# The up weights of an expert in two transfers of 4 MB, in place of four of 2 MB

## The reference

```python
def expert_block(args):            # for each expert with its tokens
    xb = t[tk]
    uu = xb @ w_up[eid] + b_up[eid]            # w_up (32, 1024, 2048)
    glu = jnp.minimum(uu[:, :D_FF], 7.0)
    lin = jnp.clip(uu[:, D_FF:], -7.0, 7.0)
    act = glu * jax.nn.sigmoid(1.702 * glu) * (lin + 1.0)
    yb = act @ w_down[eid] + b_down[eid]       # w_down (32, 1024, 1024)
    return yb * wt[:, None]
```

## Time and profile before

| | |
|---|---|
| time, median of 3 runs (lowest to highest) | 1246.54 us (1245.84 to 1250.47) |
| the profiled execution's own time | 1254.68 us |
| its span, first to last instruction | 1252.9 us |
| mean granted TensorE clock | 0.971 |
| TensorE busy | 1187.5 us, 95% of the span |
| VectorE, ScalarE, GpSimd busy | 408.7, 303.2, 36.5 us |
| moved by DMA | 442.27 MB, 353 GB/s over the span |
| queue q1 (SyncE), q10 (ScalarE) | 312.75 MB, 125.85 MB |

### The profile page before, as it was taken

How to read it: one execution, slowest core, us unless ns; L and a number is a source line. 1 busy time by engine, 2 the same in 40 slices (tenths; PEclk the granted TensorE clock), 3 DMA queues, 4 the chain that set the end, 5 groups by cost and what they waited for, 6 DMA issues and landing times.

```text
span 1252.9 us, 14792 instructions
## 1 busy us (share of the span) xinstructions
PE 1187.5 (95%) x5802; PEld 574.4 (46%) x5802; DVE 408.7 (33%) x732; ACT 303.2 (24%) x479; POOL 36.5 (3%) x90
## 2 busy tenths in 40 slices
PE   5999999998999999999999999899998999999984
PEld 3788879896333333333333333333333333333321
DVE  3543676723223132332313133132223131313233
ACT  6454244513111112111111221111111111111212
POOL 2001600000000000000000000000000000000000
PEclk9899999997999999999999999999999999999996
DMA  8650515368899999999999999999999999999971
GB/s 304 225 206 1 168 37 185 135 269 338 354 387 431 426 427 429 431 428 427 427 428 431 429 428 427 428 429 430 428 427 428 428 431 427 428 427 427 429 331 43
DMA packets 49841, 442.27 MB, mean 353 GB/s; under 512 B 3915, under 2 KB 16787, under 8 KB 25200
## 3 DMA queue, kind: packets, MB, share of 16 engines
q1 hardware_dynamic: 40032, 312.75, 60.6%
q10 hardware_dynamic: 8720, 125.85, 23.6%
q0 software_dynamic: 1056, 3.21, 0.7%
HBM read 438.06 MB, written 3.73 MB: 353 GB/s over the span
## 4 chain that ended last, share of the span: by engine, by line
PE 90%; DMA 3%; DVE 2%; ACT 1%; another core or an unknown queue 1%; issue 1%; POOL 0%; SPq 0%; DVEq 0%; POOLq 0%
PE ps L443 35%; PE ps L457 18%; PE ps L333 15%; PE ps L420 7%; DMA regionB<-in_w_up 3%; PE ps L464 2%; PE ps L450 2%; PE ps L465 2%; PE ps L426 1%; PE ps L435 1%; PE ps L1712 1%; PE ps L1497 1%; PE ps L1669 1%; PE ps L1728 1%
## 5 line engine op out<-in xcount | busy, mean ns | idle before, releaser
L443 PE MATMUL ps<-regionB,regionP 128*64 128x512 f32 x1024 | 243.2, 618 | 14.1 <-DMA regionB<-in_w_up 14.1
L443 PE MATMUL ps<-regionA,regionP 128*64 128x512 f32 x1024 | 225.9, 598 | 6.5 <-DMA regionA<-in_w_up 5.6
L457 PE MATMUL ps<-regionD,regionP 128*64 128x512 f32 x992 | 224.7, 595 | 0.0
L701 DVE TENSOR_TENSOR regionP<-ps,regionP 128x512 f32<-128x512 f32 x32 | 22.1, 691 | 403.6 <-PE ps L426 403.6
L443 PEld LDWEIGHTS ps<-regionA,regionP 128*64 128x64 f32 x1024 | 72.1, 137 | 149.0 <-issue 138.0
L443 PEld LDWEIGHTS ps<-regionB,regionP 128*64 128x64 f32 x1024 | 70.0, 141 | 150.9 <-issue 133.6
L457 PEld LDWEIGHTS ps<-regionD,regionP 128*64 128x64 f32 x992 | 68.5, 137 | 129.6 <-issue 129.5
L695 DVE SCALAR_TENSOR_TENSOR roundedP<-regionP,roundedP 64x512 fp32r<-64x512 f32 x64 | 45.2, 746 | 183.4 <-ACT roundedP L594 183.4
L420 PE MATMUL ps<-regionP 128*64 128x512 f32 x384 | 90.5, 607 | 2.4 <-ACT regionP L1153 2.4
L609 ACT ACTIVATE regionP<-ps 128x512 f32<-128x512 f32 x31 | 18.5, 597 | 298.8 <-PE ps L420 298.8
L735 DVE TENSOR_TENSOR regionP<-ps,regionP 128x1024 f32<-128x1024 f32 (+1 forms) x48 | 58.5, 1219 | 97.1 <-PE ps L465 84.9
(11 more groups left out here) (280 smaller groups left out, 1165.6 us busy)
## 6 DMA issues: line engine op xcount, KB each, us to landing
regionA<-in_w_up SPq DMA_DIRECT2D x64, 2048.0 KB, 41.9
regionB<-in_w_up SPq DMA_DIRECT2D x64, 2048.0 KB, 42.0
regionD<-in_w_down ACTq DMA_DIRECT2D x60, 2048.0 KB, 14.4
regionA<-in_w_in SPq DMA_DIRECT2D x4, 2048.0 KB, 14.1
regionB<-in_w_mk SPq DMA_DIRECT2D x4, 1024.0 KB, 9.2
regionD<-in_w_mv SPq DMA_DIRECT2D x4, 1024.0 KB, 21.6
regionD<-in_w_out SPq DMA_DIRECT2D x4, 1024.0 KB, 12.9
regionD<-in_w_mq SPq DMA_DIRECT2D x4, 1024.0 KB, 5.0
```

The costliest lines, as they stand in the source:

```text
L443: ins = pe.matmul(ps[64 * half:64 * half + 64, n_, :], XTe[:, k % 4, k // 4, :], w[:, k, 1024 * half + 512 * n_:1024 * half + 512 * n_ + 512],
L457: ins = pe.matmul(ps[64 * n_:64 * n_ + 64, 6, :], lin[:, k, :], w[:, k, 512 * n_:512 * n_ + 512], start=(k == 0), stop=(k == KT - 1))
```

## The change

The loads of an expert's up weights are issued in halves: four blocks of rows each, 4 MB, which are 32 KB for every partition, in place of four pieces of two blocks, 2 MB and 16 KB. A half is issued when both chunks that read its place are done, and TensorE waits for a half before its first chunk of the two. The wait on `down_done` before the last expert's pieces is gone. The loads ahead of the loop keep their four pieces, but two of them count on one semaphore, so that TensorE waits for 32 there. The overflow part is changed in the same way.

```diff
@@ moe_sync
-                for c_ in range(4):
-                    if isinstance(e, int) and e == E - 3 and c_ == 1:
-
-                        sp.wait_ge(S("down_done"), e * 2)
-                    sp.wait_ge(S("up_done"), e * 4 + c_ + 1)
-                    sp.dma_start((upA, upB)[h][:, 2 * c_:2 * c_ + 2, :], up_src(e + 2)[:, 2 * c_:2 * c_ + 2, :]
+                for c_ in range(2):
+                    sp.wait_ge(S("up_done"), e * 4 + 2 * c_ + 2)
+                    sp.dma_start((upA, upB)[h][:, 4 * c_:4 * c_ + 4, :], up_src(e + 2)[:, 4 * c_:4 * c_ + 4, :]
                                  ).then_inc(S(f"up{'AB'[h]}_in{c_}"), 16)
...
@@ moe_tensor
                 for c_ in range(4):
-                    pe.wait_ge(S(f"up{'AB'[h]}_in{c_}"), (pair + 1) * 16)
+                    if c_ % 2 == 0:
+                        pe.wait_ge(S(f"up{'AB'[h]}_in{c_ // 2}"), (pair + 2) * 16)
                     up_product(pe, (upA, upB)[h], 2 * c_, 2).then_inc(S("up_done"), 1)
...
@@ sync
             def load_up0(i):
-                load(upA[:, 2 * i:2 * i + 2, :], up_src(0)[:, 2 * i:2 * i + 2, :], f"upA_in{i}")
+                load(upA[:, 2 * i:2 * i + 2, :], up_src(0)[:, 2 * i:2 * i + 2, :], f"upA_in{i // 2}")
...
             for i in range(4):
-                load(upB[:, 2 * i:2 * i + 2, :], up_src(1)[:, 2 * i:2 * i + 2, :], f"upB_in{i}")
+                load(upB[:, 2 * i:2 * i + 2, :], up_src(1)[:, 2 * i:2 * i + 2, :], f"upB_in{i // 2}")
```

More of the change, by code:

```diff
@@ L395, in moe_sync @@
                 with sp.Fori(0, E) as e:
-                    for c_ in range(4):
+                    for c_ in range(2):
                         sp.wait_ge(S("up_done"), (E + e * (NBLK - 1)) * 4)
-                        sp.dma_start(upA[:, 2 * c_:2 * c_ + 2, :], up_src(e)[:, 2 * c_:2 * c_ + 2, :]
+                        sp.dma_start(upA[:, 4 * c_:4 * c_ + 4, :], up_src(e)[:, 4 * c_:4 * c_ + 4, :]
                                      ).then_inc(S(f"upA_in{c_}"), 16)
@@ L560, in moe_tensor @@
                     for c_ in range(4):
-                        if b == 1:
-                            pe.wait_ge(S(f"upA_in{c_}"), (PAIRS + 1 + e) * 16)
+                        if b == 1 and c_ % 2 == 0:
+                            pe.wait_ge(S(f"upA_in{c_ // 2}"), (PAIRS + 2 + e) * 16)
                         up_product(pe, upA, 2 * c_, 2).then_inc(S("up_done"), 1)
```

## The result

The changed kernel takes 1283.69 us (median of 4 runs, 1279.22 to 1289.05); beside it the kernel before took 1248.51 (4 runs, 1245.84 to 1254.52). The ratio is 1.0285, 95% interval 1.0255 to 1.0315: slower, by 35 us, where 16 were forecast. The profiled execution of the changed kernel took 1279.22 us (span 1277.5, mean granted clock 0.967); that of before 1254.68.

The account below looks back on a forecast made before the run. DMA engines at 428 GB/s bound the loop once up weights loaded ahead are spent. +18.3 us for thirteen pairs and −2.3 for the tail made +16: 1270.7 profiled, 1262.5 us as median, range 1246 to 1273.

Parts of the forecast that it names:

- Longer runs, one packet, 10 ns saved: Up loads: a 32 KB run staying one packet saves 10 ns, 0.3 us a pair, so 58.95 becomes 58.6 us.
- Turns by packet, two thirds for the up queue: DMA engines: queues take turns by packet, so the up queue gets two to one wherever both have work.
- Second down halves late, first ones and up weights in time: Region D: second half 8.7 and 3.8 us late in alternate iterations, first in time; waits some 30 to 45 us.
- The pair settles at the engines' own 58.6: Expert loop: up loads fill their buffers and run thin, so each pair takes 58.6 us, the engines' pace.
- the forecast's +18.3: Expert loop: thirteen pairs go from 743.5 us to 761.8 at 58.6 us each.
- The rival "worse": Engines run dry while TensorE waits for region D, slower chunks adding 20 us, 1282.5 us; chance 0.09.
- That the stock can't be spent from the start: Expert loop: region D's lateness, same in every pair, keeps early pairs from using up weights loaded ahead; 58.6, not 55.13 us.
- a sign of being wrong: Expert loop: pairs still at 55 us before 700 us would show the forecast wrong.
- Waiting for 4 MB at no cost: TensorE's coarser waits cost nothing where up weights are early; SyncE issues 60 transfers fewer on a queue that waits anyway.
- The hold: SyncE's 23.6 us wait before the last expert's second piece: the queue was backlogged, so its removal gives nothing.
- the tail: Last expert: early up weights save 3.8 us, a late down half costs 1.5, so −2.3 us.
- Profile to median: Whole kernel: the profiled execution lay 8.1 us above the runs' median, so 1270.7 became 1262.5 us.

Follow-up runs that it names:

- e4: Changed kernel with the second up half issued only when the first half of the running down load has landed; ratio 1.0109 to the kernel before.
- e11: Changed kernel with the second down half loaded by GpSimd's queue, all partitions, the first staying on ScalarE's; ratio 0.9989 to the kernel before.
- e1: Changed kernel with 4 MB up transfers kept but made of blocks lying apart, so runs are 16 KB; ratio 1.0027 to the kernel before.
- e2: Kernel before with only the down weights changed, to runs of 8 KB beside the up weights' 16 KB; ratio 1.0171.
- e6: e2 with TensorE alone waiting for two up pieces before the first of two chunks, loads still issued piece by piece; ratio 1.0180 to the kernel before.
- e5: e1 and e2 together: up transfers of 4 MB in runs of 16 KB, down weights in runs of 8 KB; ratio 1.0245 to the kernel before.
- e3: Changed kernel with the wait on the down products put back ahead of the last expert's second half; ratio 1.0252 to the kernel before.
- e8: Kernel before with up weights in runs of 8 KB, down weights still in 16 KB; ratio 1.0087.
- e9: Changed kernel with each down half split by partitions between ScalarE's queue (0 to 63) and GpSimd's (64 to 127); ratio 1.3805 to the kernel before.

## Why the prediction was right in kind, and the step in which its size failed

Two terms make the pace, and both can be read off before and after. *Rate*: 25.17 MB at 428 GB/s is 58.8 us; at the 424 of after, 59.4. *Stock*: before the loop ran ahead of its rate by 58.8 − 57.2 = 1.6 us a pair, 21 us in all, on up weights loaded ahead.

- **Longer runs, one packet, 10 ns saved:** right. Where the engines never run dry 32 KB runs give 431 and 430 GB/s (e4, e11) in place of 428; that is the forecast's 58.6, within 0.1 us.
- **Turns by packet, two thirds for the up queue:** right (191 and 181 packets, 5.73 and 2.70 MB), and it is the cause of the loss: undoing it by the run's length (e1), or by a third queue with all else kept (e11), takes the loss away, and making it in the kernel before (e2) brings about half of it, its own shorter packets taken off.
- **Second down halves late, first ones and up weights in time:** right in kind and in sum. 42.3 us before the down products (30 to 45 forecast), none before the up products, the late halves landing up to 28.2 us after issue (25 to 30). Wrong in how often: the forecast took the distance to late as the same in every pair, and the late half as the rule. Eight second halves in the whole loop were late, and once it has settled one in four. After a long wait the up queue is empty, the next second half lands in 12 us (issued at 801.0, landed at 812.8), and the pair that follows runs at 55.13 us.
- **"The pair settles at the engines' own 58.6":** this is the step that failed. It took the engines as always full, and put the time that they stand at nothing. The mean pair takes 59.66: 13 × (59.66 − 58.6) = 13.8 us more than the forecast's +18.3. The rate makes 10 of the 13.8 us: 59.4 us a pair at 424 GB/s in place of 58.6. Of these 10 the slow first packets behind the long waits are 7.3 by the records, the standing engines the rest. The remaining 3 to 4, pace above rate, were not traced further. The rival "worse" had the engines running dry, but it got 0.09 of the chance, placed the dry time in the wait itself (it comes behind it), and priced the slow chunk alone, 1.5 us in each pair; that its 1282.5 us lies near the 1283.69 measured is luck. The slower half after a wait costs TensorE 2.0 us (16.0 in 8 waits). It lies ahead of the issue at 811.54, so it may lengthen the dry time; no run tested how much.
- **That the stock can't be spent from the start:** right in the mean; the first six pairs took 58.8 us each against 55.13, though no single one of them took 58 to 59, and one, from 593.46 us, still took 55.13, which the prediction had named as a sign of being wrong. e4 comes nearest to the forecast's own regime, full engines and down weights late in 19 short waits, and its pace of 58.0 gives 13 × (58.0 − 57.2) = +10 us, 1.0109 in time. There some of the stock is spent; that the forecast would have been too high with full engines is argued from this, since e4 also delays an up load.
- **Waiting for 4 MB at no cost:** right for TensorE's wait (e6 against e2), wrong for the issue. That SyncE issues after two chunks rather than one was taken as harmless "on a queue that waits anyway". After a long wait for region D that queue runs empty before two chunks have gone by to feed it again, and engines stand (279 GB/s): e5 against e2, 0.7%.
- **The hold, the tail:** right. e3 shows no worth of the hold, and the end shrank by 3.4 us (−2.3 forecast).
- **Profile to median:** the 8.1 us taken off as if profiled executions ran above their median was no constant: the changed kernel's ran 4.5 us below. These 12.6 us and the missing 13.8, less the 4.2 of the earlier start and 1.1 of the tail, are the 21.1 between 1262.5 and 1283.69 but for rounding; together they put the time above the range's 1273.

What stays open: that the coarse issue and the two to one make more together (1.0245) than their sum (1.0198) is shown as a rate for e5 (424 GB/s against e2's 426); the single waits were followed in the changed kernel only, and the later issue was not run apart from the larger transfer.

## What to carry to other kernels

Where queues share the DMA engines, turns are counted in packets and a run is a packet: before lengthening the runs of one queue, look at the least slack of the loads on the others and work out their landing at the new share. If the longer runs are wanted, give the other side as many queues as keep its share of bytes. And when a load becomes late, ask next whether the DMA engines still have work until the next load is issued: here that issue hung on the engine that had waited, by a coarser step than before.

## What the runs showed of the hardware

- A run of 32 KB stays one packet: 191 packets for 5.73 MB, and 10 ns fixed for each packet fit 424, 428 and 430 GB/s for up runs of 8, 16 and 32 KB (e8, before, e11).
- Three queues, one of them software, take equal turns: 106, 112 and 94 packets (e11), 51, 50 and 50 (e9).
- The first packet of 32 KB on each engine, when an up load met an empty queue and engines that had begun to stand, took 1.84 us, against 1.21 in a full queue.
- While loads into half of the partitions from two queues ran beside a full load (e9), each packet took 1.7 to 1.8 times as long (2.02 us for 32 KB, 1.11 for 16 KB), and the rate was 243 GB/s. What in the chip does this was not tried.
